# Sample values in four column groups, and expert queries from rounded parts

## What is computed

```
s = q k^T * scale + c[t] - c[s];  p = softmax(mask(s));  out = p v      # FoX head group, 8 heads of 64
q = (h2 @ w_pq).reshape(rows, 8 heads, 256);  q = q * rsqrt(mean(q*q) + eps)
s1, s2 = q[:128] . sub_keys[0],  q[128:] . sub_keys[1]                  # 128 keys each
top 16 of each, top 16 of their 256 sums, softmax -> gates of 16 experts per head
y = sum over chosen experts of gelu(u_e . h2) * gate * v_e
```

## Time and profile before

| What | Value |
|---|---|
| median of the runs | 1978.99 us |
| the profiled execution's own time | 1977.69 us |
| its span, first to last instruction | 1975.6 us |
| TensorE matmul busy | 1814.0 us, 92% |
| VectorE busy | 1585.1 us, 80% |
| ScalarE, GpSimd busy | 789.2 us, 969.8 us |
| mean granted TensorE clock | 0.95 of 2.4 GHz |

### The profile page before, as it was taken

How to read it: one execution, slowest core, us unless ns; L and a number is a source line. 1 busy time by engine, 2 the same in 40 slices (tenths; PEclk the granted TensorE clock), 3 DMA queues, 4 the chain that set the end, 5 groups by cost and what they waited for, 6 DMA issues and landing times.

```text
span 1975.6 us, 28032 instructions
## 1 busy us (share of the span) xinstructions
PE 1814.0 (92%) x9103; PEld 1494.5 (76%) x9103; DVE 1585.1 (80%) x3300; ACT 789.2 (40%) x1291; POOL 969.8 (49%) x779
## 2 busy tenths in 40 slices
PE   6999899999994878629999999999999999999998
PEld 4883554566653867619999999999999999999997
DVE  5306462366558799998999999999999999999999
ACT  4311651221213556624443444344434443444443
POOL 0004000022223020347777777777777777777773
PEclk8999999988876999869999999999999999999999
DMA  6110303323120544439999999999999999999996
GB/s 244 43 63 2 128 1 122 119 94 99 36 79 22 174 146 160 146 125 403 415 410 403 391 397 408 401 394 392 410 399 390 401 410 392 396 397 409 394 395 275
DMA packets 169002, 517.83 MB, mean 262 GB/s; under 512 B 18128, under 2 KB 51856, under 8 KB 164848
## 3 DMA queue, kind: packets, MB, share of 16 engines
q0 software_dynamic: 73728, 268.47, 34.2%
q1 hardware_dynamic: 70448, 223.46, 29.8%
q10 hardware_dynamic: 24768, 25.17, 3.7%
HBM read 486.20 MB, written 30.84 MB: 262 GB/s over the span
## 4 chain that ended last, share of the span: by engine, by line
PE 79%; DVE 15%; ACT 4%; issue 2%; DMA 1%; SPq 0%; ACTq 0%; DVEq 0%
PE ps L1244 27%; PE ps L1260 9%; PE ps L1262 9%; PE ps L1261 9%; PE ps L1136 5%; PE ps L1109 3%; DVE asel L1532 2%; DVE bsel L1525 2%; PE ps L953 2%; PE ps L954 2%; PE ps L955 2%; PE ps L1183 1%; PE ps L1085 1%; PE ps L1060 1%; PE ps L1151 1%
## 5 line engine op out<-in xcount | busy, mean ns | idle before, releaser
L624 POOL DMA_INDIRECT ubuf<-in_peer_u,ix x256 | 386.3, 1509 | 156.0 <-POOL ix L669 109.0
L624 POOL DMA_INDIRECT vbuf<-in_peer_v,ix x256 | 406.7, 1588 | 78.9 <-issue 77.7
L1260 PE MATMUL ps<-hh,uh 128*128 128x384 f32 x1024 | 345.0, 337 | 18.9 <-DVEq L1621 18.9
L1262 PE MATMUL ps<-hh,ul 128*128 128x384 f32 x1024 | 345.8, 338 | 0.0
L1261 PE MATMUL ps<-hl,uh 128*128 128x384 f32 x1024 | 344.7, 337 | 0.0
L1633 DVE SCALAR_TENSOR_TENSOR ubuf<-ubuf,h2Y 128x1024 f32<-128x1024 f32 x256 | 303.0, 1222 | 4.0 <-DMA ubuf<-in_peer_u,ix 3.3
L899 ACT ACTIVATE vh<-vb 128x1024 fp32r<-128x1024 f32 x128 | 136.0, 1062 | 294.7 <-PE ps L1244 286.4
L1244 PE MATMUL ps<-vl,acth 128*128 128x512 f32 x774 | 243.1, 395 | 0.0
L1244 PE MATMUL ps<-vh,actl 128*128 128x512 f32 x774 | 242.3, 394 | 0.0
L1244 PE MATMUL ps<-vh,acth 128*128 128x512 f32 x774 | 242.1, 393 | 0.0
L1260 PEld LDWEIGHTS ps<-hh,uh 128*128 128x128 f32 x1024 | 194.4, 190 | 25.5 <-issue 19.7
(11 more groups left out here) (359 smaller groups left out, 2869.8 us busy)
## 6 DMA issues: line engine op xcount, KB each, us to landing
ub<-in_peer_uT SPq DMA_DIRECT2D x130, 512.0 KB, 6.8
vb<-in_peer_v SPq DMA_DIRECT2D x129, 512.0 KB, 6.6
gbuf<-gate_matrix SPq DMA_DIRECT2D x68, 384.0 KB, 8.2
gate_matrix<-stage ACTq DMA_DIRECT2D x12, 2048.0 KB, 7.7
wpqX<-in_wpq SPq DMA_DIRECT2D x8, 1024.0 KB, 4.9
wpqY<-in_wpq SPq DMA_DIRECT2D x8, 1024.0 KB, 5.0
w_oX<-in_w_o SPq DMA_DIRECT2D x4, 1024.0 KB, 7.8
kTs<-in_past_k SPq DMA_DIRECT2D x8, 512.0 KB, 4.0
```

The lines of the kernel that those rows point to most:

```text
L624: nc.gpsimd.indirect_dma_start(out=dst[slot][:, e, :], out_offset=None, in_=t_in[table], in_offset=bass.IndirectOffsetOnAxis(ix[:, slot, e ...
L1260: mm(ps[:, 6 + slot, 0:NTD], uh[slot][:, k], hh[:, k], start=(k == 0), stop=False)
L1262: last = mm(ps[:, 6 + slot, 0:NTD], ul[s][:, k], hh[:, k], start=False, stop=(k == KD - 1))
```

## The change

FoX values of a sample: the 32 columns of turned probabilities of one head pair become the weights, the 128 value columns move, and the result lands in 32 rows of the bank, one column group of the array for each pair c; c is now the inner loop. The result then has its rows and columns the other way round, so ScalarE copies it (`copy_rows`) and TensorE turns it (`turn_rows`) between the two halves of a later head's queries, and `copy_out` waits for that.

Queries of the dense tiles: `h2TX` is gone. ScalarE rounds the turned rows straight from PSUM into `hh` and VectorE takes the low parts into `hl`. ScalarE rounds each half of the query weights (`round_weights`), VectorE takes its low part in place (`low_weights`), and TensorE adds three fp32r products. `hh` and `hl` of the dense loop are these same tiles, so L872 and its subtraction go. `copy_out` moves from 8 items of `half_choices` to 14. SBUF addresses are laid out anew.

```diff
+            def copy_rows(b):
+                act.wait_ge(pv_done, FIRST + b + 1)
+                if b >= 1:
+                    act.wait_ge(rows_turned, b)
+                A(rowS[:], out_cols(FIRST + b, 0), ACT.Copy).then_inc(rows_copied, 1)
...
+                    if g == 0:
+                        A(hh[:, 4 * q:4 * q + 4, at * P:(at + 1) * P],
+                          ps[:, 4 + q].rearrange("p (c k) -> p c k", c=4), ACT.Copy).then_inc(hh_ready, 1)
+                        continue
...
+            def round_weights(h, c):
+                act.wait_ge(wpq_loaded[h % 2], 16 * (h // 2 + 1))
+                if h >= 1:
+                    act.wait_ge((wpq_used, pq_done)[c], h)
+                feats = slice(c * P, (c + 1) * P)
+                A(wpq_hi[:, :, feats], GR[0].wpq[h % 2][:, :, feats], ACT.Copy).then_inc(wpq_rounded, 1)
+
             for t in TILES[0]:
+                if t == 2:
+                    round_weights(0, 0)
+                    round_weights(0, 1)
                 root_norm(t)
                 copy_turned(t)
             for h in range(PH):
+                if h + 1 < PH:
+                    round_weights(h + 1, 0)
                 copy_queries(0, h)
+                if h + 1 < PH:
+                    round_weights(h + 1, 1)
                 if h >= 1:
                     copy_transposed(FIRST + h - 1)
                 copy_scores(0, h)
                 exponentials(FIRST + h)
+                if h >= 1:
+                    copy_rows(h - 1)
             copy_transposed(ALL - 1)
+            copy_rows(DB - 1)
...
-            A(hh[:], GR[0].h2T[:], ACT.Copy).then_inc(hh_ready, 1)
...
-                for c in range(4):
-                    for k in range(3):
+                for k in range(3):
+                    for c in range(4):
...
-                        mm(out_cols(n, 0)[:, 32 * c:32 * c + 32], v, probTS[rows, 0, k * P + 32 * c:k * P + 32 * c + 32],
+                        mm(out_cols(n, 0)[32 * c:32 * c + 32], probTS[rows, 0, k * P + 32 * c:k * P + 32 * c + 32], v,
                            start=(k == 0), stop=(k == 2))
...
+            def turn_rows(b):
+                pe.wait_ge(rows_copied, b + 1)
+                tr(out_cols(FIRST + b, 0), rowS[:], ident[:]).then_inc(rows_turned, 1)
...
+                    if c == 1 and between is not None:
+                        between()
...
+                        if g == 0:
+                            if k == 0:
+                                pe.wait_ge(wpq_split, 2 * h + c + 1)
+                            hi, lo = wpq_hi[:, k, feats], wpq_lo[h % 2][:, k, feats]
+                            mm(out[:, c], hi, hh[:, k], start=(k == 0), stop=False)
+                            mm(out[:, c], hi, hl[:, k], start=False, stop=False)
+                            last = mm(out[:, c], lo, hh[:, k], start=False, stop=(k == KD - 1))
...
-                queries(0, h)
+                queries(0, h, (lambda: turn_rows(h - 2)) if h >= 2 else None)
...
             project_out(TD)
+            turn_rows(DB - 2)
             transpose_probabilities(ALL - 1)
             sample_values(DB - 1)
+            turn_rows(DB - 1)
...
-                dve.wait_ge(pv_done, n + 1)
+                dve.wait_ge(rows_turned, c + 1)
...
-            for t in TILES[0]:
-                norm(t)
...
+            norm(0)
+            norm(1)
+            low_turned(0)
+            norm(2)
+            low_turned(1)
+            low_weights(0, 0)
+            low_turned(2)
+            low_weights(0, 1)
...
             row_max(FIRST)
+            low_weights(1, 0)
             normalise(FIRST)
+            low_weights(1, 1)
             for h in range(1, PH + 1):
                 items = half_choices(0, h - 1)
-                some(items, 8)
+                some(items, 14)
                 if h >= 2:
                     copy_out(FIRST + h - 2)
-                some(items, 12)
+                if h + 1 < PH:
+                    low_weights(h + 1, 0)
+                some(items, 6)
                 if h < PH:
                     row_max(FIRST + h)
                 some(items, 4)
                 if h < PH:
                     normalise(FIRST + h)
+                if h + 1 < PH:
+                    low_weights(h + 1, 1)
                 finish(items)
...
-            low_part(hl[:], GR[0].h2T[:], hh[:], hh_ready, 1, hl_ready)
```

More of the change, by code:

```diff
@@ L178, in peer_step_kernel @@
         latT = tile("latT", [P, MH, P])
+        rowS = tile("rowS", [P, P])
         lfs = tile("lfs", [P, L])
@@ L210, in group @@
                 [tile(f"w_o{tag}{k}", [P, 2, D]) for k in range(4)],
-                tile("x2" + tag, [P, n, D]), tile("h2T" + tag, [P, KD, n * P]),
+                tile("x2" + tag, [P, n, D]), tile("h2T" + tag, [P, KD, n * P]) if g else None,
                 [tile(f"wpq{tag}{k}", [P, KD, 2 * P]) for k in range(2)],
@@ L224, in peer_step_kernel @@
         assert TK * TK <= 2 * CAND
+        wpq_hi = tile("wpqh", [P, KD, 2 * P], F32R)
+        wpq_lo = [tile(f"wpql{k}", [P, KD, 2 * P], F32R, at=f"wpqX{k}") for k in range(2)]
         gffn = tile("gffn", [P, D])
@@ L1122, in transpose_h2, with queries @@
                     last.then_inc(h2t_done, 1)
-            def queries(g, h):
+            def queries(g, h, between=None):
                 x, out = GR[g], query_bank(g, h)
-                pe.wait_ge(wpq_loaded[h % 2], 16 * (PH // 2 * g + h // 2 + 1))
+                if g == 1:
+                    pe.wait_ge(wpq_loaded[h % 2], 16 * (PH // 2 + h // 2 + 1))
                 if h == 0:
@@ L1134, in queries @@
                 for c in range(2):
+                    if c == 1 and between is not None:
+                        between()
                     for k in range(KD):
-                        last = mm(out[:, c], x.wpq[h % 2][:, k, c * P:(c + 1) * P], x.h2T[:, k, :],
-                                  start=(k == 0), stop=(k == KD - 1))
+                        feats = slice(c * P, (c + 1) * P)
+                        if g == 0:
[5 more added lines that the diff above has]
+                            last = mm(out[:, c], lo, hh[:, k], start=False, stop=(k == KD - 1))
+                        else:
+                            last = mm(out[:, c], x.wpq[h % 2][:, k, feats], x.h2T[:, k, :],
+                                      start=(k == 0), stop=(k == KD - 1))
+                    if g == 0 and c == 0:
+                        last.then_inc(wpq_used, 1)
                 last.then_inc(pq_done, 1)
@@ L1543, in _, with low_turned, low_weights @@
                     copy_out(n_ - 4)
-            for t in TILES[0]:
-                norm(t)
+            def low_turned(t):
+                for q in range(2):
+                    at = (slice(None), slice(4 * q, 4 * q + 4), slice(t * P, (t + 1) * P))
+                    low_part(hl[at], ps[:, 4 + q].rearrange("p (c k) -> p c k", c=4), hh[at],
+                             hh_ready, 2 * t + q + 1, h2t_copied)
+            def low_weights(h, c):
+                at = (slice(None), slice(None), slice(c * P, (c + 1) * P))
+                low_part(wpq_lo[h % 2][at], GR[0].wpq[h % 2][at], wpq_hi[at], wpq_rounded, 2 * h + c + 1, wpq_split)
+            norm(0)
[6 more added lines that the diff above has]
+            low_weights(0, 1)
             dve.wait_ge(keys_loaded, 32)
```

29 lines of the change are left out of this document (16 added, 13 removed), and 19 rows, old and new, of the table AT.

## The result

The changed kernel takes 1963.01 us (median of 3 runs, 1960.73 to 1963.72); the kernel before took 1978.99. The ratio is 0.991 (95% interval 0.9894 to 0.9927). The forecast was 1963.7. The profiled execution took 1963.01 as well, with a span of 1961.2 us, so against the profiled execution of before 14.7 us are gone (1977.69 less 1963.01); the working summed to 15.3.

A forecast was written before the change was run, and what follows sets the result against it. VectorE was taken to release TensorE late once in two rounds. Start 5.0, pairs 5.7, end of loop -1.2, tail -0.3 and split 6.05 summed to 15.3 us saved: 1963.7 us, range 1951 to 1975.

The forecast's parts named there:

- Start of the loop: From the first query product to the end of queries 2, forecast at 400.5: 5.0 us saved.
- The stall: TensorE's wait for `copy_out` after a pair: restart 33.2 us after the even queries' end, stall 12.8 us instead of 2.4.
- three signs of being wrong: Stalls under 8 us in rounds 3, 5 and 7; stalls in even rounds; a changed length of the stage 624 to 890.
- Behind the stall: Restart to next even queries' end: 15.3 us at full clock, 22.0 at half, middle 18.7; period 51.9, 5.7 saved over two.
- end of the loop: From the last even queries' end to the loop's end: 41.9 us instead of 40.7, 1.2 lost.
- FoX values: A sample's FoX value block on TensorE: 1.4 us instead of 3.79, bounds 0.95 and 3.79; latent values 1.9.
- Tail and split: Behind the loop, copies and turns lose 0.3 us; removing `hh` and `hl` behind `turn_choices` saves 6.05.
- VectorE isn't in the way: Rival in the head loop: TensorE's whole gain shows, 57 us less, 1922; chance 0.03.
- clock comes back at once: Rival in the head loop: the clock holds or returns at once, 25.2 us less, 1953.8; chance 0.14.
- half clock behind every stall: Rival in the head loop: TensorE at half clock after each stall, 5 us less, 1974; chance 0.12.
- No overlap: Rival on the FoX values: column groups don't overlap, 2.4 us for each of five blocks, 12 us back, 1976; chance 0.05.
- The slower rival: Rounded queries don't raise the clock behind each round; a head's queries take 17.3 us, end near 2020; chance 0.04.

The follow-up runs named there:

- group_outer: The changed kernel with column groups in the outer loop of the FoX values, so successive products go to the same group: 1977.49 us.
- split_back: The changed kernel with the rounding copy and the subtraction of the rows put back behind `turn_choices`, on scratch data: 1969.29 us.
- copy_at_8: The changed kernel with `copy_out` back after 8 items instead of 14: 1949.98 us.
- queries_alone: The changed kernel with the FoX values of before; rounded queries and the later `copy_out` stay: 1987.48 us, ratio 1.005 to the kernel before.
- before_decoding: The changed kernel with VectorE's order rebuilt: `copy_out` inside the pair, `normalise` and a low part ahead of its last two items: 1933.92 us.
- float32_split_ahead: The kernel before with turned FoX values, VectorE's order rebuilt, float32 queries, and the rows' rounding ahead of the copies of `turn_choices`: 1923.34 us.
- no_low_weights: The changed kernel without VectorE's low parts of the query weights; the third product reads the rounded weights again: 1952.81 us.
- values_alone: The kernel before with the new FoX values, two turns and the later `copy_out`; queries stay float32, split behind `turn_choices`: 1962.22 us.

## Why the prediction was right, and where its account was wrong

**Start of the loop: right.** Predicted 356.3 for the first product, 377.3 for the second half of queries 1, 400.5 for the end of queries 2; measured 357.13, 378.56 and 400.30. Saved 5.15 for 5.0. It hit with errors against each other: queries 1 ended 1.4 us late (the wait for `low_weights(1, 1)`), and queries 2 took 0.8 longer (0.50 of it a wait for a low part); from there to queries 2 it was 1.3 shorter (FoX and latent values), and the 1.1 us priced in for the clock behind sample 0 did not come.

**The stall: right to its steps.** Predicted 12.92 to the pair, 27.15, 32.3 and 33.2; measured 12.84, 27.06, 32.19 and 33.08 to 33.45. The stalls of 13.06, 13.11 and 12.64 are the forecast 12.8. `low_weights(h+1, 0)` beside the decoding took 1.59 and 1.58 us, so the 3 us that were allowed for it did not come either. None of the three signs of being wrong appeared: the stalls are longer than 8 us, in even rounds there is none ahead of the turned probabilities, and the stage to the dense loop takes 262.5 us before and after.

**Behind the stall: the middle of two outcomes.** The periods are 49.4 and 54.1; each of the two forecasts of 51.9 missed by 2.2 to 2.5, and their sum, 103.8, met 103.5. The ends of the range, 48.5 (clock back at once) and 55.2 (half clock), describe the rounds better than its middle does. The last round went the second way: 43.3 us where 41.9 was forecast, so the end of the loop lost 2.6 instead of 1.2. That the middle met the sum is luck: it is the mean of rounds that went one way or the other, and no row of before said how many would go which way.

**FoX values: mis-sized.** 1.4 us forecast, 0.92 measured, just under my lower bound of 0.95. The instances ahead of a stall are hidden by it. The Trainium skill's 4x column tiling behind a swap of the operands (TensorEngine Tiling (Array Packing), § Performance Considerations) fits the trace, 3.79 / 0.92 = 4.1, with the groups in turn. In group_outer, with the same operands, the factor is 1.07. The latent values were mis-sized too: I kept 1.9 us, which in the earlier trace rows were taken partly at half clock; at full clock they are 1.06 (389.82 to 390.88).

**Tail and split.** Tail: 0.3 lost was forecast, 1.0 was gained (the project_out of the last tile starts 9.6 us earlier, the loop ends 8.6 earlier). Split: 6.05 forecast, 5.9 in the chain and 6.3 by split_back. At the gates 15.5 us were gone for the forecast 15.3; at the end of the execution 14.7 of it. The total was met to 0.7 us, closer than the method allows: end of the loop 1.4 worse, tail 1.3 better, the rest within 0.3, and single executions of the kernel before lie 10 us apart.

**The step that failed: what pays for it.** The text says that VectorE's 2.44 us a head "is where the change pays", but the sum never set this against what the cheaper queries bring; it credits the loop's gain to both edits. The single edits say otherwise. The new values, with the later `copy_out`, gave the whole 15 us. The rounded queries, with the later `copy_out`, lost 10, of which that later place is some 8: behind the old values and behind each stall they run at half clock, and VectorE sets the restart 33.1 us after the even queries, as in the changed kernel. On top of the new values they cost 3.4 us in the loop and returned 6 behind it, with no difference in the total that these runs resolve. The TensorE time that they free ahead of a restart, 2 us a head, falls into the stall. The forecast also left out that `copy_out` behind 14 items instead of 8 is a part of the change with a price of its own: it counted 2.7 us a round correctly, but did not say that undoing it alone would give the 8 us back (copy_at_8, which measured 13, some 5 of them with the clock).

**The rivals.** "VectorE isn't in the way" (1922) is refuted by the stalls. Of "clock comes back at once" and "half clock behind every stall" each was right for one or two rounds. "No overlap" was false for this kernel and describes group_outer. Its 1976 against 1977.5 measured is a near hit by another sum: it priced five blocks at 2.4 us and no clock, and the trace shows the clock in it. The slower rival, that rounded queries don't raise the clock, is refuted by round 5, where it came back inside them, some 15 us behind the restart.

**Open.** Why the clock came back 4 us behind a stall of 13.06 us and not for 15 us behind one of 13.11 isn't settled; split_back, with stalls of 13.09, 13.09 and 12.67, went the same way round by round. The length of the stall doesn't decide alone: behind the 6.9 of queries_alone and the 6.67 of group_outer it came back only after some 19 us.

## What to carry to other kernels

Follow a saving to the engine that releases the next step: while VectorE's pair of choices stood ahead of one copy of 0.44 us, TensorE's savings became a stall, and rebuilding VectorE's order around that copy (30 us in the medians with float32 queries) was worth more than both edits. Compare executions with the same mean clock where it wanders: by that two of the gains above, 13 and 9.6 us, come down to some 8 and 3. A split into rounded parts moves work from TensorE to the engine that makes the parts, so it pays only where that engine has slack: with VectorE's order rebuilt, rounded and float32 queries came out within 2 us of each other. With column groups, put the group in the inner loop.

## What the runs showed of the hardware

- Twelve products of four column groups took 0.92 us in turn and 3.54 group by group. The Trainium skill (TensorEngine Tiling (Array Packing), § Key Properties) says that different tiles can run in parallel, and that a change of mode drains the engine. The trace agrees with the first: twelve products in 0.92 us. The 0.92 us includes the changes of mode on both sides; whatever such a drain costs, it is small beside the gain.
- VectorE's two TENSOR_SCALAR of 128x272 took 5.19 us beside GpSimd's L602 instead of 0.63. The low part of 128x1024 took 3.83 beside the decoding in before_decoding and 1.59 in the changed kernel, instead of 1.22. The other way round, GpSimd's three L603 took 8.17 us instead of 5.15 with VectorE's subtraction of 128x3072 beside them (float32_split_ahead).
- Values with 32 moving columns: in all ten blocks of the loop that started at a granted clock of 1.00 (six of the kernel before, four of queries_alone) it was 0.50 directly behind them, though TensorE was busy for the whole 3.50 us before (queries_alone). With 128 moving columns and the groups in turn it fell there in 11 of 25 (the changed kernel 1 of 5, copy_at_8 2 of 7, no_low_weights 3 of 6, values_alone 5 of 7), with the groups one after the other in 1 of 5 (group_outer).
- After a stall of 6 us or more the granted clock is 0.50. In the kernels with the groups in turn it was back at 1.00 within some 4 us of the restart in all eight rounds with stalls of 9 to 11.2 us (copy_at_8, values_alone, no_low_weights), and in two of the seven with 12.6 to 13.1 (the changed kernel and split_back, round 3 of each); in the other rounds of the changed kernel and in no_low_weights it took some 15 us. In the two kernels whose value products don't alternate it took 19 us in five of six rounds (all three of queries_alone, two of group_outer) and 5 in the last (group_outer, stall of 11.61). The value products start 4.8 us or later behind a restart, and what stands ahead of them is the same in all these kernels, so their form can't by itself explain a return within 4 us.
